# The last expert task of a mixture-of-experts layer: leaving out the weight loads for the task after it

## The reference

```
logits = h @ w_r + b_r
top_v, top_i = top_k(logits, 2)
gate = softmax(top_v)
comb = sum_k gate[k] * one_hot(top_i[k], 8)
for e in range(8):
    out += comb[..., e] * (silu(h @ w_gate[e]) * (h @ w_up[e])) @ w_down[e]
h = layer_norm(ALPHA * h + out)
```

## Time and profile before

| | us |
|---|---|
| median of 3 runs | 1942.2 (1940.83 to 1942.74) |
| the profiled execution | 1937.77 |
| its span, first to last instruction | 1936.2 |
| stage of the expert tasks, TensorE from the first to the last product (lines 1825 and 1846) | 1304.8 to 1888.6 |
| from the last product to the end of the span | 47.6 |

### The profile page before, as it was taken

One profiled execution on the slowest core, in us unless ns is written; L12 is line 12 of the kernel. 1 busy time (PEld: TensorE's weight loads), 2 busy tenths in 40 slices (PEclk: granted clock), 3 DMA queues, 4 the chain that ended last, 5 costly groups with the idle time before them and its releaser, 6 DMA issues.

```text
span 1936.2 us, 28354 instructions
## 1 busy us (share of the span) xinstructions
PE 1750.3 (90%) x10485; PEld 1493.9 (77%) x10485; DVE 1329.2 (69%) x2137; ACT 962.4 (50%) x1289; POOL 51.5 (3%) x74
## 2 busy tenths in 40 slices
PE   5998788979999999988997798969999999999990
PEld 4997455869999999978984456848888888888880
DVE  6795667454544454467975765468888888888886
ACT  4334665233121212223335664148888888888872
POOL 0000000000000000000000000020000000000002
PEclk9999787789999999998998877989999999999995
DMA  3740011112222222215420211258999999999996
GB/s 150 204 143 23 23 66 44 41 47 66 87 88 70 84 88 88 66 44 132 130 86 23 82 32 47 83 222 326 378 380 379 379 377 380 379 379 379 378 378 216
DMA packets 74019, 337.17 MB, mean 174 GB/s; under 512 B 16194, under 2 KB 29186, under 8 KB 55554
## 3 DMA queue, kind: packets, MB, share of 16 engines
q1 hardware_dynamic: 65250, 308.42, 43.2%
q0 software_dynamic: 6800, 23.38, 3.6%
q10 hardware_dynamic: 1872, 4.06, 0.5%
HBM read 317.04 MB, written 22.85 MB: 176 GB/s over the span
## 4 chain that ended last, share of the span: by engine, by line
PE 79%; DVE 14%; ACT 3%; issue 2%; DMA 1%; POOL 0%; ACTq 0%; DVEq 0%; SPq 0%
PE ps L1526 31%; PE ps L1825 19%; PE ps L1846 9%; DVE x L1052 3%; PE ps L1663 2%; PE ps L1509 2%; PE ps L1562 2%; PE ps L1683 2%; PE ps L1497 2%; PE ps L1633 1%; PE ps L1549 1%; PE ps L1645 1%; ACT parena L800 1%; DVE parena L1006 1%; PE ps L1831 1%
## 5 line engine op out<-in xcount | busy, mean ns | idle before, releaser
L789 ACT ACTIVATE w_high<-w 128x1024 fp32r<-128x1024 f32 x82 | 87.0, 1061 | 266.7 <-PE ps L1526 265.4
L1825 PE MATMUL ps<-mixed_high,hidden_low 128*128 128x512 f32 x576 | 189.7, 400 | 2.5 <-DVE hidden_low L1403 2.5
L1825 PE MATMUL ps<-h_high,hidden_low 128*128 128x512 f32 (+1 forms) x576 | 161.3, 358 | 0.3 <-DVE w_high L1398 0.3
L1526 PE MATMUL ps<-h_low,w_high 128*128 128x288 f32 x672 | 143.7, 295 | 0.0
L1526 PE MATMUL ps<-h_high,w_low 128*128 128x288 f32 x672 | 143.7, 295 | 0.0
L1526 PE MATMUL ps<-h_high,w_high 128*128 128x288 f32 x672 | 143.6, 295 | 0.0
L1284 DVE TENSOR_TENSOR parena<-parena,ps 128x576 f32<-128x576 f32 x22 | 16.6, 754 | 184.7 <-PE ps L1526 181.7
L902 ACT ACTIVATE mixed_high<-w 128x2048 fp32r<-128x2048 f32 x74 | 139.2, 1913 | 8.1 <-DMA w<-in_moe_gu 5.7
L1526 PE MATMUL ps<-hidden_low,w_high 128*128 128x288 f32 x608 | 131.8, 298 | 0.0
L1825 PEld LDWEIGHTS ps<-mixed_high,hidden_low 128*128 128x128 f32 x576 | 109.2, 190 | 28.7 <-issue 2.6
L1052 DVE SCALAR_TENSOR_TENSOR x<-uext,par,x 128x512 f32<-128x512 f32 x240 | 124.4, 518 | 8.6
(11 more groups left out here) (352 smaller groups left out, 4036.9 us busy)
## 6 DMA issues: line engine op xcount, KB each, us to landing
w<-in_moe_gu SPq DMA_DIRECT2D x63, 2048.0 KB, 7.9
carena<-in_moe_dn SPq DMA_DIRECT2D x50, 1024.0 KB, 7.4
w<-in_split_w SPq DMA_DIRECT2D x82, 512.0 KB, 3.6
w<-in_w_in SPq DMA_DIRECT2D x32, 512.0 KB, 4.2
bias<-in_moe_dn SPq DMA_DIRECT2D x13, 1024.0 KB, 8.9
w<-in_moe_gu_last SPq DMA_DIRECT2D x12, 1024.0 KB, 8.1
parena<-sorted_rows POOLq DMA_DIRECT2D x12, 512.0 KB, 10.0
bias<-in_moe_dn SPq DMA_DIRECT2D x12, 512.0 KB, 10.9
```

The lines of the kernel that those rows point to most:

```text
L789: done(nc.scalar.activation(piece_parts[p % 4][0], piece_raw[p % 4], ACT.Copy), w_high)
L1526: last = M(PS[0:rows, b + n, 0:HALF], w, act_[:, cols], start=(i == j == 0), stop=(i == len(steps) - 1 and j == 2))
L1825: last = M(PS[:, 2 + c % 2, 0:n], x_[:, k, :], w[:, k, :], start=(k == j == 0), stop=(k == KD - 1 and j == 2))
```

## The change

VectorE writes one more integer into the table, entry 35, which is T - 1. SP reads this number instead of T as `final`. The body of its loop becomes a function `loads(t, more)`; the loop runs it `final` times with all twelve loads, and behind the loop it stands once more, for t = `final`, with the five loads behind down 4 left out. The loops of the other engines still run T rounds.

```diff
-        TASK = sb("task", 2 * NT + 1, rows=1, dt=I32)
+        TASK = sb("task", 2 * NT + 2, rows=1, dt=I32)
...
             sp.wait_ge(task_ready, 1)
-            T = sp.value_load(TASK[0:1, 2 * NT:2 * NT + 1], min_val=1, max_val=NT)
-            with sp.Fori(0, T) as t:
+            final = sp.value_load(TASK[0:1, 2 * NT + 1:2 * NT + 2], min_val=NE - 1, max_val=NT - 1)
+
+            def loads(t, more):
                 e = sp.value_load(TASK[0:1, bass.ds(t, 1)], min_val=0, max_val=NE - 1)
                 e_next = sp.value_load(TASK[0:1, bass.ds(t + 1, 1)], min_val=0, max_val=NE - 1)
                 load_up(e, 3, t)
...
                 load_down(e, 3, t)
                 load_up(e_next, 0, t + 1)
                 load_down(e, 4, t)
-                load_up(e_next, 1, t + 1)
-                load_up(e_next, 2, t + 1)
-                load_down(e_next, 0, t + 1)
-                load_down(e_next, 2, t + 1)
-                load_down(e_next, 1, t + 1)
+                if more:
+                    load_up(e_next, 1, t + 1)
+                    load_up(e_next, 2, t + 1)
+                    load_down(e_next, 0, t + 1)
+                    load_down(e_next, 2, t + 1)
+                    load_down(e_next, 1, t + 1)
+
+            with sp.Fori(0, final) as t:
+                loads(t, True)
+            loads(final, False)
...
-            num = RT[0:1, 800:800 + 2 * NT + 1]
+            num = RT[0:1, 800:800 + 2 * NT + 2]
...
             done(V.tensor_copy(num[:, 2 * NT:2 * NT + 1], ce[0:1, NE - 1:NE]))
+            done(V.tensor_scalar(num[:, 2 * NT + 1:2 * NT + 2], ce[0:1, NE - 1:NE], -1.0, None, ALU.add))
             done(V.tensor_copy(TASK[:, :], num), task_ready)
```

## The result

| | before | after |
|---|---|---|
| median | 1938.29 us (13 runs, 1935.14 to 1943.30) | 1931.95 us (13 runs, 1926.05 to 1936.03) |
| the profiled execution | 1937.77 | 1933.1 |
| its span | 1936.2 | 1931.6 |
| last expert product to the end of the span | 47.6 | 43.4 |

The three runs from which the prediction started are among the 13 before. The ratio of the changed kernel to the one before is 0.9966, with a 95% interval of 0.9952 to 0.9979: faster by 0.34%, 4.1 to 9.3 us. The prediction gave 1937.7 with a range of 1936.0 to 1940.5. The profiled execution came out almost where it was forecast for one: 1931.6 and 1933.1 us against 1931.7 and 1933.3.

A forecast was written before the change was run, and what follows sets the result against it. TensorE was taken to bound the tasks, with a chain of waits through the last store behind them. Terms 0 + 0 - 4.5 us, set against the 1942.2 us median, gave 1937.7 us, range 1936.0 to 1940.5.

The forecast's parts named there:

- What bounds the kernel: Expert tasks: TensorE works without a gap and sets the pace, so fewer bytes in a round would by themselves give nothing.
- The store: Last task's result store: without the five loads ahead it lands in 2.6 us instead of 7.12, gaining 4.5 us.
- Case B: Last store: gets engines at once but has a larger fixed part on ScalarE's queue, lands in 3.2 to 3.9 us; chance 0.18.
- Case C: Last store: the wait belongs to ScalarE's queue, not SP's loads, so 7.12 us stay, total 1942.2; chance 0.05.
- the upper bound: Last store: POOL's same store amid busy engines lands in 3.8 us, so the gain is at least 3.3 us.
- The gathers keep their shape: Tail behind the store: POOL's gathers and VectorE's sums move forward by the store's gain, with no second gain.
- Case E: Tail: gathers also start on quieter memory and land sooner, 1 to 2 us on top, total 1936.2; chance 0.07.
- VectorE's instruction: Table stage before the first product: the added instruction takes 0.18 us on VectorE, cost to the kernel 0.
- the cover of 0.50 us: Before TensorE's first product: VectorE's 0.50 us wait for ScalarE hides the added instruction; without it the cost is 0.2 us.
- The last round behind the loop: SP's code after its loop: 6.7 us of slack, 2.3 us of it for two table reads, so cost 0.
- Rival D: SP's code behind the loop must first be fetched through full engines; 2.0 us slower, total 1944.2; chance 0.04.
- How the numbers follow: Whole-kernel time: weighing of the cases, with chance 0.67 of faster and range 1936.0 to 1940.5 us.

The follow-up runs named there:

- e4: Changed kernel with the last round's loads up 1 and up 2 kept, only the three down pieces left out; store lands in 2.70 us, span 1925.3 us.
- e7: Kernel before with all its loads, only the last store issued by POOL instead of ScalarE; store lands in 6.90 us, span 1937.8 us.
- e12: Changed kernel with VectorE's added instruction done twelve times; span 1932.4 us.
- e8: Changed kernel with eight more table reads by SP ahead of up 3 of the last round; span 1935.0 us.
- e3: Changed kernel run again without edit; median 1934.85 us over 12 runs, ratio 0.9977 to the kernel before.
- e10: Changed kernel run a third time without edit; median 1932.42 us over 12 runs, ratio 0.9974 to the kernel before.
- e2: Changed kernel with all twelve loads issued in the last round; median 1937.88 us over 12 runs, ratio 0.9993 to the kernel before.
- e1: Kernel before against itself, no edit; median 1934.2 us over 12 runs, ratio 0.998.
- e9: Kernel before against itself again, no edit; median 1938.8 us over 12 runs, ratio 1.0001.
- e6: Changed kernel with the five loads kept but held back until the last product is done; store lands in 11.15 us, span 1943.6 us.
- e5: Changed kernel with the last round's three down loads kept, up 1 and up 2 left out; store lands in 5.21 us, span 1933.1 us.

## Why the prediction was right, and where it was wrong

**What bounds the kernel: right.** TensorE ends the last task without a gap with the loads and without them; from the first to the last expert product took 583.8 us before, 584.0 after, and 583.3 to 585.0 in all the runs. 7.3 MB less in the last round moved nothing there.

**The store: right, in mechanism and size.** Forecast 2.6 us, measured 2.70, 2.69, 2.70. Of the 4.4 us that it loses to the loads, 2.8 lie before its first packet (3.65 us after the issue, 0.87 on idle engines) and 1.6 behind it, where the queues share. The row of the output stores on idle engines was the right one, and SP's queue or ScalarE's made at most 0.1 us of difference. Case B (3.2 to 3.9 us) is refuted, and with it the estimate of 3.2 us from the Trainium skill's "DMA: Bandwidth & Descriptors" ("Anatomy of one DMA"), a fit for POOL's transfers. Case C is refuted by e4: the same store on the same queue lands in 2.70 us. But one argument for the upper bound was weaker than it looked: the 3.8 us of POOL's stores were read as those of a store among full engines, and e7 measured 6.90 for such a store.

**The gathers keep their shape: right.** From the first gather to VectorE's first sum were 7.02 us before and 6.95 after; to the second sum, by which the chain goes in both kernels, 10.13 and 10.27. Case E, a second gain of 1 to 2 us there, did not come.

**VectorE's instruction: the cost right, the cover not always there.** It costs 0.18 us. The prediction took 0 from the cover of 0.50 us and named 0.2 us as the price without it; six profiles have no cover, and e12 shows that added time then arrives at the last product. That the change costs nothing even so is luck as far as the prediction goes: the cast of 36 numbers is 0.17 us shorter than that of 35, which nothing in it foresaw, so 0.01 us is left.

**The last round behind the loop: right that it costs nothing, with a wrong figure in it.** A read was put at 1.15 us from VectorE's wait; e8 shows 0.67 at most. Rival D did not happen: up 3 of the last task comes in time in every run. Something small did change. In the changed kernel one instruction fetch lies in the last round, in 1855 to 1856,

```profile
q14 instruction: 1, 0.01, 1.9%
```

and down 5 is issued 6.61 us after up 3 instead of 6.20, in the changed kernel and in every run with that code except e8. These 0.4 us delay nobody: the load behind it comes 11.46 us after up 3 and 11.45 before the change. The fetch shown comes after the delay, so it is not its cause, and e8 has a fetch in its last round as well (in 1849 to 1850) and no delay. The cause is open.

**How the numbers follow: this step failed.** "The gain is set against the median: 1942.2 - 4.5 = 1937.7", with a range of "a microsecond of spread". The 1942.2 were three runs. Over 13 runs the same kernel has 1938.29, over 29 in the next job 1937.5, over 23 in the third 1938.2. Of the 5.75 us between forecast and measurement 3.9 are this. The prediction had the warning in hand: it noted that the profiled execution took 1937.8, 4.4 us less than the median, and took the median all the same. The remaining 1.8 us are the difference between a gain of 4.5 and 6.3 in these medians. The range failed with it, and not by the reference alone: moved down by those 3.9 us it would reach from 1932.1 to 1936.6, and 1931.95 is still below. A microsecond, or the 1.9 us over three runs, was too little for the spread of a kernel whose runs lie up to 14 us apart. The three ratios of the changed kernel (gains of 6.6, 4.5 and 5.0 us) have intervals 5 to 8 us wide that all hold 4.5, and the traces have 4.7 from the last product on. Between runs of like granted clock in the same job the medians differ by 4.4 us (0.936 and more) and 1.9 (below) for e3, and by 3.2 and 5.5 for e10. I count the 1.8 us as spread; that they are is argued, not shown.

Where the spread comes from can be seen in part. The first expert product starts between 1299.0 us (e4) and 1307.7 (e2) in traces of kernels that are the same up to there but for one small instruction, while behind it all of them agree within 2 us. The granted clock goes with it. Ahead of the first expert product TensorE stands at the lower of its two levels (1.2 GHz) for 201 us in e4 and for 222 us in e2, and none of the twelve other profiles lies outside these two in either number. The clock of the whole span shows it less cleanly, since TensorE is at the lower level in the tail too, and a shorter tail raises the mean: it is 0.937 for e4, whose run took 1926.87 us, and 0.931 for e2's profile. Among the 13 runs of the changed kernel the four below 1929 us have 0.936 or 0.937, the other nine 0.931 to 0.934. So the spread of the traces is made before the expert tasks and goes with the clock that TensorE is granted there. What sets the clock, and whether the changed code has any part in it, no run shows.

## What to carry to other kernels

Transfers that nobody reads are not free when they are issued last: look what is issued within the next microseconds behind them, above all a store on which the tail waits. What such a transfer costs is not its bytes but the part of them that the engines still move before the store has landed, so the last ones matter and the early ones may stay. And a forecast of an absolute time is no better than its reference: with three runs of a kernel whose runs spread over 14 us, the distances within a trace are known to half a microsecond while the total is not known to 3.

## What the runs showed of the hardware

- A store that is issued while SP's queue holds all 16 engines moves nothing at first. Its first packet comes 3.65 us after the issue in the kernel before, 3.78 in e1, 3.67 in e9, 3.77 in e2, 3.97 in e6 and 4.25 from POOL's queue (e7), against 0.87 us on idle engines (after); in e5, where SP's queue has only 1.2 MB left, it comes after 2.93. In the six SP's queue moves 1.4 MB until then (1.6 in e7), in packets of 8 KB as of 16 KB. What makes this delay is not shown.
- After it, two queues that both have work take turns, one packet each (34 and 33 in the kernel before, 59 and 56 in e6), so the store with its 4 KB packets gets a third of the bytes beside packets of 8 KB and a fifth beside packets of 16 KB. Two queues with work did not get equal halves of the bytes. The Trainium skill ("DMA: Bandwidth & Descriptors", "Queues, rings and completion order") says that each engine takes turns between its rows packet by packet, a packet being some 9 to 17 descriptors. The turns are there in the profile's packets, but the first 4 us don't look like them, and whether the profile's packets are those of the page no run here shows.
- VectorE's cast of 35 numbers from float32 to int32 on one partition takes 0.33 to 0.34 us, that of 36 takes 0.17. It is so in all 14 traces. An even count may be the reason; no run tried another.
- 512 KB from SBUF to DRAM on idle engines: 2.6 us from SP's queue and 2.7 from ScalarE's, as 128 rows of 4 KB; 256 KB as 128 rows of 2 KB, beside the other half: 2.16 us.
